# One core, a two-block transformer: reordered expert routing, deferred down biases, and unused matrix products in TensorE's waits

## The reference, cut to what matters

```
logits = xt @ w_router + b_router            # 256 tokens x 32 experts
top_v, top_i = top_k(logits, 4);  gates = softmax(top_v)
for each expert e and its tokens:
    hdn = xb @ w_gate_up[e] + b_gate_up[e]   # 1024 -> 2048
    y   = clamped_swiglu(hdn) @ w_down[e] + b_down[e]
out[token] += gate * y
```

## Time and profile before

| what | us |
|---|---|
| median of 3 runs | 1916.14 |
| lowest and highest of them | 1914.5 and 1930.97 |
| the profiled execution, its own time | 1931.54 |
| its span, first to last instruction | 1929.6 |
| PE busy | 1808.8 (94%) |
| PE weight loads busy | 1064.2 (55%) |
| DVE busy | 629.0 (33%) |
| ACT busy | 456.3 (24%) |
| mean granted clock, share of full | 0.964 |
| HBM read | 557.12 MB |

### The profile page before, as it was taken

The page is one execution under the profiler, slowest core; times in us unless marked ns, Lnnn a source line. Parts: engine busy times, 40 slices in busy tenths (PEclk is TensorE's granted clock), DMA queues, the critical chain, the costliest instruction groups (busy, mean ns, idle before and its releaser), DMA issues.

```text
span 1929.6 us, 21825 instructions
## 1 busy us (share of the span) xinstructions
PE 1808.8 (94%) x8533; PEld 1064.2 (55%) x8533; DVE 629.0 (33%) x941; ACT 456.3 (24%) x615; POOL 121.7 (6%) x207
## 2 busy tenths in 40 slices
PE   7979999899899999999799999999999999989997
PEld 6756888777578877875533333333333333333333
DVE  3376666526666664121311100111111110111011
ACT  3363343315443423232101101111000111101011
POOL 1021111101111111001000000000000000000000
PEclk9989999899999998967699999999999999999999
DMA  7324777541367666431299999799999899999995
GB/s 287 131 66 147 240 237 262 185 157 62 109 210 253 228 247 211 174 131 44 96 419 429 428 429 428 305 423 428 429 428 420 312 423 429 429 428 428 428 429 241
DMA packets 116217, 559.12 MB, mean 290 GB/s; under 512 B 7428, under 2 KB 52768, under 8 KB 91416
## 3 DMA queue, kind: packets, MB, share of 16 engines
q1 hardware_dynamic: 105968, 526.66, 67.8%
q0 software_dynamic: 9536, 31.42, 5.3%
q10 hardware_dynamic: 648, 0.14, 0.0%
HBM read 557.12 MB, written 1.06 MB: 289 GB/s over the span
## 4 chain that ended last, share of the span: by engine, by line
PE 72%; DMA 14%; issue 6%; DVE 4%; ACT 3%; POOL 1%; ACTq 0%; POOLq 0%; DVEq 0%; SPq 0%
PE PA L1801 12%; DMA ring<-w_down 12%; PE PB L1801 9%; PE PA L1841 5%; PE PB L1841 4%; PE PA L1432 4%; PE PC L1432 2%; PE PA L1631 2%; PE PD L1631 2%; PE PD L1632 2%; PE PA L1632 2%; PE PD L1638 2%; PE PA L1638 2%; PE PC L1886 2%; DMA prob<-w_ada 2%
## 5 line engine op out<-in xcount | busy, mean ns | idle before, releaser
L1801 PE MATMUL PB<-ring,arena 128*64 128x512 f32 x1088 | 240.8, 594 | 18.5 <-DMA ring<-w_gate_up 18.5
L1801 PE MATMUL PA<-ring,arena 128*64 128x512 f32 x1088 | 238.2, 594 | 0.0
L990 DVE TENSOR_TENSOR ring_rounded<-ring,ring_rounded 128x4096 fp32r<-128x4096 f32 (+2 forms) x48 | 191.0, 3980 | 109.0 <-ACT ring_rounded L705 109.0
L1801 PEld LDWEIGHTS PB<-ring,arena 128*64 128x64 f32 x1088 | 76.7, 137 | 178.6 <-issue 142.5
L705 ACT ACTIVATE ring_rounded<-ring 128x4096 fp32r<-128x4096 f32 (+2 forms) x48 | 156.8, 3271 | 66.7 <-PE PD L1668 33.9
L1801 PEld LDWEIGHTS PA<-ring,arena 128*64 128x64 f32 x1088 | 76.6, 137 | 148.4 <-issue 148.4
L1841 PE MATMUL PA<-ring,arena 128*64 128x512 f32 x544 | 132.5, 596 | 16.6 <-DMA ring<-w_down 16.6
L895 ACT ACTIVATE gla<-gla 128x512 f32<-128x512 f32 x34 | 21.4, 630 | 522.9 <-DVE gla L1346 522.9
L1841 PE MATMUL PB<-ring,arena 128*64 128x512 f32 x544 | 131.4, 592 | 0.0
L1346 DVE TENSOR_SCALAR gla<-PA 128x512 f32<-128x512 f32 x17 | 11.8, 692 | 337.0 <-PE PA L1811 337.0
L1362 DVE COPY arena<-PB 128x512 f32<-128x512 f32 x17 | 11.8, 692 | 243.0 <-PE PB L1841 243.0
(11 more groups left out here) (413 smaller groups left out, 2715.7 us busy)
## 6 DMA issues: line engine op xcount, KB each, us to landing
ring<-w_gate_up SPq DMA_DIRECT2D x128, 2048.0 KB, 17.3
ring<-w_down SPq DMA_DIRECT2D x64, 2048.0 KB, 22.3
ring<-w_in SPq DMA_DIRECT2D x36, 1024.0 KB, 7.3
prob<-w_ada POOLq DMA_DIRECT2D x96, 256.0 KB, 3.7
ring<-w_gate SPq DMA_DIRECT2D x22, 1024.0 KB, 7.3
ring<-w_up SPq DMA_DIRECT2D x22, 1024.0 KB, 9.7
ring<-w_down SPq DMA_DIRECT2D x14, 1024.0 KB, 8.2
ring<-w_out SPq DMA_DIRECT2D x12, 1024.0 KB, 6.3
```

Of the source, the lines that this page charges most:

```text
L990: v.tensor_tensor(rest, w, rounding, ALU.subtract).then_inc(S_["w_fine"], 1)
L1801: last = mm((PA, PB)[x][h * SLOTS:(h + 1) * SLOTS, u, :], XT[:, c, x * SLOTS:(x + 1) * SLOTS], ring[:, slot, at:at + BANK], start=c == 0, ...
```

## The change

Four things are changed. On DVE, `MASK` is reduced over 32 columns and the three further copies are made by a copy; the block that makes flags and rank rows moves ahead of the gates; the gates' reduction is cut in the same way; a semaphore `gated_rows` now tells TensorE that the gates are there. On ACT, PC and PD are set to zero (a copy with scale 0) after `ROWS` is taken, with a semaphore `sums_zeroed`. The four down-bias products move from the front of the first gather to the place behind the first loop of mixed pairs, with `start=False`. And `keep_busy` puts 29 products of 128x128 by 256 columns, whose result nobody reads, into TensorE's program at eight places. The list of semaphore names at the top, in which the two new ones are entered, is left out here.

```diff
--- before.py
+++ after.py
...
@@ -877,6 +877,10 @@
             for t in range(T):
                 last = A_(PROBS(t), TOP(t)[:, 0:TOPK], ACT.Exp, bias=TSUM(t, 0), accum_out=TSUM(t, 1))
             last.then_inc(top_exp, 1)
+            act.wait_ge(*upto("ht_act", L, 4 + 2 * T))
+            for t in range(T):
+                last = A_(banks((PC, PD)[t]), K[:, 0:D], ACT.Copy, scale=0.0)
+            last.then_inc(sums_zeroed, 1)
             act.wait_ge(parted_t, 1)
             A_(PARTED.rearrange("p u s -> p (u s)"), PB[:, 1, :], ACT.Copy).then_inc(parted, 1)
 
@@ -1269,10 +1273,29 @@
                 last = v.tensor_tensor(HOT(t), times(k_("iota")[:, 0:NE], 1, TOPK), times(TOPF(t), 2, NE), ALU.is_equal)
             then(L, last)
             for t in range(T):
-                last = v.tensor_reduce(MASK(t).rearrange("p (r e) -> p r e", e=NE),
-                                       times(HOT(t).rearrange("p j e -> p e j"), 1, PARTS), X_AXIS, ALU.add)
+                last = v.tensor_reduce(MASK(t)[:, 0:NE], HOT(t).rearrange("p j e -> p e j"), X_AXIS, ALU.add)
+            then(L, last)
+            for t in range(T):
+                last = v.tensor_copy(MASK(t)[:, NE:P].rearrange("p (r e) -> p r e", e=NE), times(MASK(t)[:, 0:NE], 1, PARTS - 1))
             last.then_inc(mask_ready, 1)
-            dve.wait_ge(mask_ready, 1)
+
+            def flags():
+
+                dve.wait_ge(mask_ready, 1)
+                dve.wait_ge(ranks_done, 1)
+                count = PA[:, 0, 2 * NE:2 * NE + 1]
+                then(L, v.tensor_tensor(OTHER[:, 0:1], count, k_("upto_full"), ALU.is_le))
+                v.scalar_tensor_tensor(FLAGS[:, 0:1], count, k_("over"), OTHER[:, 0:1], ALU.is_gt, ALU.mult)
+                v.tensor_tensor(FLAGS[:, 1:2], count, k_("over_full"), ALU.is_gt).then_inc(flags_ready, 1)
+                for t in range(T):
+                    last = v.scalar_tensor_tensor(RK[:, t, 0:NE], PA[:, 0, t * NE:(t + 1) * NE], 1.0, MASK(t)[:, 0:NE], ALU.add, ALU.mult)
+                then(L, last)
+                for t in range(T):
+                    for r in range(1, PARTS):
+                        last = v.tensor_scalar(RK[:, t, r * NE:(r + 1) * NE], RK[:, t, 0:NE], float(-r * SLOTS), None, ALU.add)
+                last.then_inc(routed, 1)
+
+            flags()
             dve.wait_ge(top_exp, 1)
             for t in range(T):
                 last = v.reciprocal(TSUM(t, 2), TSUM(t, 1))
@@ -1284,24 +1307,13 @@
                 last = v.tensor_tensor(HOT(t), HOT(t), times(PROBS(t), 2, NE), ALU.mult)
             then(L, last)
             for t in range(T):
-                last = v.tensor_reduce(GATE[:, t, :].rearrange("p (r e) -> p r e", e=NE),
-                                       times(HOT(t).rearrange("p j e -> p e j"), 1, PARTS), X_AXIS, ALU.add)
+                last = v.tensor_reduce(GATE[:, t, 0:NE], HOT(t).rearrange("p j e -> p e j"), X_AXIS, ALU.add)
             then(L, last)
-            dve.wait_ge(ranks_done, 1)
-
-            count = PA[:, 0, 2 * NE:2 * NE + 1]
-            then(L, v.tensor_tensor(OTHER[:, 0:1], count, k_("upto_full"), ALU.is_le))
-            v.scalar_tensor_tensor(FLAGS[:, 0:1], count, k_("over"), OTHER[:, 0:1], ALU.is_gt, ALU.mult)
-            v.tensor_tensor(FLAGS[:, 1:2], count, k_("over_full"), ALU.is_gt).then_inc(flags_ready, 1)
-            for t in range(T):
-                last = v.scalar_tensor_tensor(RK[:, t, 0:NE], PA[:, 0, t * NE:(t + 1) * NE], 1.0, MASK(t)[:, 0:NE], ALU.add, ALU.mult)
-            then(L, last)
-            for t in range(T):
-                for r in range(1, PARTS):
-                    last = v.tensor_scalar(RK[:, t, r * NE:(r + 1) * NE], RK[:, t, 0:NE], float(-r * SLOTS), None, ALU.add)
-            last.then_inc(routed, 1)
+            for t in range(T):
+                last = v.tensor_copy(GATE[:, t, NE:P].rearrange("p (r e) -> p r e", e=NE), times(GATE[:, t, 0:NE], 1, PARTS - 1))
+            last.then_inc(gated_rows, 1)
+
             dve.wait_ge(routed, 1)
-
             dve.wait_ge(places_done, 1)
 
             then(L, v.tensor_copy(PLACES, PB[:, 0, 0:4]))
@@ -1377,6 +1389,11 @@
         @block.tensor
         def _(pe):
             mm = nc.tensor.matmul
+
+            def keep_busy(bank, n):
+
+                for _ in range(n):
+                    mm(bank[:, 0:S], ident, k_("cos_q"), start=True, stop=True)
 
             def weights(l, i):
 
@@ -1742,7 +1759,9 @@
             attend(L, 2 * AH - 1, attention(2 * AH - 1)[2], PB)
             project_out(L)
             for t in range(T):
+                keep_busy(PB[:, 1, :], (0, 3)[t])
                 transpose_rows(L, t)
+                keep_busy((PB, PA)[t][:, 1, :], (9, 3)[t])
                 pe.wait_ge(*upto("ht_act", L, 4 + t + 1))
                 pe.wait_ge(*upto("ht_dve", L, 4 + t + 1))
                 for c in range(KD):
@@ -1755,6 +1774,7 @@
                     last = nc.tensor.transpose(banks((PC, PD)[t])[:, c * P:(c + 1) * P], HT[:, c, t * P:(t + 1) * P], ident)
                 last.then_inc(S_[("transposed_a", "transposed_b")[t]], 1)
 
+            keep_busy(PA[:, 1, :], 3)
             pe.wait_ge(mask_ready, 1)
             mm(PA[:, 0, 0:NE], k_("before"), MASK(0)[:, 0:NE], start=True, stop=True)
             mm(PA[:, 0, NE:2 * NE], ones[:, :], MASK(0)[:, 0:NE], start=True, stop=False)
@@ -1768,6 +1788,8 @@
             mm(PB[:, 0, 1:2], k_("before_pair"), FLAGS[:, 1:2], start=True, stop=True)
             mm(PB[:, 0, 2:4], ones[:, :], FLAGS, start=True, stop=True).then_inc(places_done, 1)
             pe.wait_ge(routed, 1)
+            keep_busy(PA[:, 1, :], 3)
+            pe.wait_ge(gated_rows, 1)
             for t in range(T):
                 nc.tensor.transpose(PB[:, 1, t * P:(t + 1) * P], RK[:, t, :], ident)
                 last = nc.tensor.transpose(PB[:, 1, S + t * P:S + (t + 1) * P], GATE[:, t, :], ident)
@@ -1784,6 +1806,7 @@
                     last.then_inc(S_["gathered"], 1)
 
             pe.wait_ge(*upto("ht_act", L, 4 + 2 * T))
+            keep_busy(PA[:, 1, :], 4)
             pe.wait_ge(parted, 1)
             pe.wait_ge(perm_ready, 1)
             for u in range(2):
@@ -1888,12 +1911,8 @@
                         if n == 1:
                             last.then_inc(S_["combined"], 1)
 
-            pe.wait_ge(narrow_loaded, 48)
-            for t in range(T):
-                for n in range(2):
-
-                    mm((PC, PD)[t][:, n, :], PARTED[0:NE, 1, t * P:(t + 1) * P], BD[:, n * BANK:(n + 1) * BANK], start=True,
-                       stop=True, skip_group_check=True)
+            pe.wait_ge(sums_zeroed, 1)
+            keep_busy(PA[:, 1, :], 4)
             gather(0, range(2))
 
             def mixed_pair(m, others):
@@ -1913,6 +1932,11 @@
 
             with pe.Fori(0, LEADS[0]) as m:
                 mixed_pair(m, 0)
+            pe.wait_ge(narrow_loaded, 48)
+            for t in range(T):
+                for n in range(2):
+                    mm((PC, PD)[t][:, n, :], PARTED[0:NE, 1, t * P:(t + 1) * P], BD[:, n * BANK:(n + 1) * BANK], start=False,
+                       stop=True, skip_group_check=True)
             with pe.Fori(0, same) as h:
                 same_pair(h, LEADS[0])
             with pe.Fori(*LEADS) as m:
```

More of the change, by code:

```diff
@@ L346, in program @@
          router_done, top_ready, top_exp, mask_ready, ranks_done, flags_ready, routed, places_done, parted_t, parted, perm_ready, items_done,
-         items_ready, bz_zeroed) = (sem(n) for n in (
+         items_ready, gated_rows, sums_zeroed, bz_zeroed) = (sem(n) for n in (
              "rel_ready small_loaded dist_done dist_copied dist_stored flipped_loaded flipped_done bias_b_ready "
@@ L351, in program @@
              "bias_f router_done top_ready top_exp mask_ready ranks_done flags_ready routed places_done "
-             "parted_t parted perm_ready items_done items_ready bz_zeroed").split())
+             "parted_t parted perm_ready items_done items_ready gated_rows sums_zeroed bz_zeroed").split())
         wfull = [sem(f"weights_loaded_{s}") for s in range(DENSE_SLOTS)]
```

## The result

| | before | changed |
|---|---|---|
| median of 20 runs, us | 1916.61 | 1909.03 |
| lowest and highest | 1913.72, 1934.55 | 1905.05, 1928.96 |
| median of the lower level | 1916.14 (13 runs) | 1908.12 (15 runs) |
| median of the upper level | 1930.57 (7 runs) | 1924.86 (5 runs) |
| profiled execution | 1931.54 | 1908.16 |

The ratio of the changed kernel to the one before is 0.9943, with a 95% interval of 0.9921 to 0.9965: 7.6 us by the medians, against 7.2 forecast, and 1909.0 was the forecast time. It is faster beyond its interval (which reaches from 6.7 to 15 us), by less than 1%. Most executions of both kernels lie near one of two levels some 15 us apart. The profile before shows an execution of the upper level, the one after an execution of the lower, so their spans (1929.6 and 1906.2) can't be compared as they stand.

A forecast was written before the change was run, and what follows sets the result against it. Bound mostly by weight DMAs at 428 GB/s, alternating with TensorE's pace. Stream start 10.6 us earlier less 3.4 for biases gives 7.2, so 1916.14 becomes 1909; range 1903 to 1925 (forecast's own 1906 to 1912).

The forecast's parts named there:

- The mechanism: Experts' weight stream: the end moves by the shift of the stream's start, plus whatever TensorE loses behind the fourth pair.
- Part 1: TensorE around the router: unused products hold the clock at full, so the router is done at 926.47 instead of 929.20, 2.7 us earlier.
- the rival without the clock: Routing stretch: clock stays as before, only the order gains; stream gains 5.7 us, less 3.4, giving 1913.8; chance 0.22.
- Part 2: DVE's mask reduction, narrowed: 0.72 plus 0.35 for copies instead of 1.98; mask at 929.6 instead of 933.24, 0.9 from this.
- Part 3: DVE's routing, flags before gates: mask to places falls from 6.2 to 5.0 to 5.2 us, 1.2 us earlier.
- Part 4: From permutation to weight stream: `items_ready` 5.7 us earlier, the 4.9 us DMA hole disappears, stream starts 10.6 us earlier.
- 3 us of room: Before the first expert pair: a slower gather could take 3 us more without delaying the stream's start.
- Part 5: Four down-bias products behind the fourth pair: nothing covers them, 3.4 us lost; bounds 0 and 7.1.
- The rule on transposes: Router stretch: transposes do not count as busy, so the clock could fall there in spite of the unused products.

## Why the prediction was right

The forecast was 1909.0 and 7.2 us; the medians say 7.6, the lower levels 8.0, the anchored ends 8.5. That the median meets 1909.0 to 0.03 us is luck: the gain of the stream was forecast 1.8 too small and the loss behind it 0.5 too small, which cancel in part; the clock did not fall behind the biases in the profiled execution; and a median depends on how many of the executions keep the attention's clock (15 of 20 here, 5 of 12 in a kernel whose end is 0.24 us earlier). Point by point:

- **The mechanism** (end = shift of the stream, plus what TensorE loses behind the fourth pair) is shown. A delay ahead of the gather reached the fourth combination (5.91 to 5.97), and the biases' place decided 3.2 us by itself. Two readings under it were wrong: the "25.17 us" that the fourth pair is said to wait are the load's, TensorE waits 4.0 there; and a gain of 0.7 at items_ready beyond the changed kernel's did not pass through.
- **Part 1, the clock,** measured 2.5 for 2.7, and carries more than the router: without the unused products the whole gain is 0.9 us (2.5 if the clock had held behind the biases, for the 2.3 of the rival without the clock).
- **Part 2, the masks,** measured 0.87 for 0.9 on each reduction; undone together they cost 1.75 to items_ready, as 27.67 against 25.92 shows. The 128-element reductions take 0.66 a pair (0.72 taken).
- **Part 3, the order,** is the step that failed, though its sum (6.2 to 5.0) measured 6.22 to 4.85. I credited 1.2 us to moving the flags. The gain is the narrower reduction, the end of the wait for ACT and the three products at full clock; the move itself costs 0.9 us while the clock holds. What it gives is a shorter wait of TensorE for the flags (0.64 against 1.67 to 2.39 us), and in three of the five profiled kernels with unused products and the longer wait the clock fell there.
- **Part 4, the stream,** was 1.8 us too small: 12.4 at the fourth combination for 10.6. A second start of the stream also loses its climb. The claimed 3 us of room was really 0.6, so the sum had no reserve where I thought it had.
- **Part 5, the biases,** was forecast at 3.4; the products took 3.63 and the tail grew by 3.9. In five of the ten profiled kernels with the products between pairs the clock fell behind them, which cost 1.3 to 1.6 us more where TensorE sets the pace. That moving them away from the front pays at all is not shown: in front they cost 3.0 with the clock held (end 0.8 earlier than changed) and 5.2 without (0.9 later). What pays is the place ahead of the fourth pair.
- **The rule on transposes:** the Trainium skill, TensorE: Matmul & The Clock Gate, Part 4, says that a transpose does not count as busy in the same way. No run here separates transposes from the products beside them, so it stays open.
- **The two levels** were taken into the range (1903 to 1925), which held both; their cause, the attention's clock, was not named.

## What to carry to other kernels

Unused products in TensorE's waits can pay (7.65 us here, for nothing where they fit) in a chain in which short steps of several engines alternate, but each group must end before TensorE's next real work is due, and at half clock it lasts nearly twice as long (2.91 against 1.56). Work that nobody needs soon belongs where its engine waits anyway, in the pair that waits for weights and not at the border to one that doesn't. Find the place by the chain of waits, but take the length of the wait from the engine's own timeline: the chain shows how long the transfer took, 25 us, where TensorE waited 4. An effect of the clock that comes in half of the executions can't be pinned on a cause by one profile against one. Before two traces are compared, find an event that both share and count from it: here most of the 23 us between the spans had nothing to do with the change.

## What the runs showed of the hardware that I had not expected

- The granted clock can fall although TensorE is never idle: 0.79 in 928 to 932 behind four 32-row products, in one execution. Behind the same four products between two pairs it fell in five of ten profiled kernels. Whether their 32 rows are the cause stays open.
- Before, the attention ran at 0.50 for 40 us with TensorE 95% busy, and took 79.0 us instead of 63.2.
- A stream of DMAs that stands still also loses 1.0 to 1.1 us at its new start, and a delay that let it stand still for 4.0 us came out as 5.97 three pairs later.
- Behind waits of TensorE of 1.68 us the clock fell in two profiled executions, and behind waits of 1.67 and 1.68 it held in two others, with the same program around them.
